# Three more chunks of an input projection as seven block products, and one block's selection moved between attention steps

## The reference, cut to what matters

```python
h = rmsnorm(x, g_mix_pre[l])
z = h @ w_in[l]                     # 1024 -> 3,908 columns
qa, ka, va, qi, ki, wi, qb, kb, vb, gb = split(z)
qa, ka, qi, ki, qb, kb = (rope(a, pos) for a in ...)
# group A, prompt, in blocks of 128 queries
sc = sum_h wi[h] * relu(qi[h] @ ki.T)          # indexer, 4 heads
sc = where(key <= query, sc, -inf)
_, sel = top_k(sc, 128)             # 128 keys for each query
a = softmax(qa @ ka[sel].T / 8) @ va[sel]      # 8 heads of 64
# group A, sample rows: the same over 256 cached keys and the new one, top 64
# group B: retention over qb, kb, vb in chunks of 128 tokens, gated by gb
x = x + rmsnorm(concat(a, b) @ w_out[l])
x = x + rmsnorm(relu(rmsnorm(x) @ w_up[l])**2 @ w_down[l])
```

## Time and profile before

| | us |
|---|---|
| median of three runs | 1571.54 |
| the profiled execution, its own time | 1573.14 |
| its span in the profile | 1571.4 |
| layer 0, start of chunk 1, and end of P7 of chunk 4 (attention begins) | 27.70, 163.06 |
| layer 0, chunk 5 ends, chunk 6 begins | 216.50 |
| layer 0, chunk 6's sample rows begin | 266.18 |
| layer 1, the same first two marks | 805.08, 942.78 |

### The profile page before, as it was taken

How to read it: one execution, slowest core, us unless ns; L and a number is a source line. 1 busy time by engine, 2 the same in 40 slices (tenths; PEclk the granted TensorE clock), 3 DMA queues, 4 the chain that set the end, 5 groups by cost and what they waited for, 6 DMA issues and landing times.

```text
span 1571.4 us, 21618 instructions
## 1 busy us (share of the span) xinstructions
PE 1547.7 (98%) x7966; PEld 1154.9 (73%) x7966; DVE 845.1 (54%) x1708; ACT 450.0 (29%) x1045; POOL 476.1 (30%) x354
## 2 busy tenths in 40 slices
PE   8999999999999999999999999999999999999998
PEld 5445755688888888888844466556888888888887
DVE  4599679846652013333467977788366610132334
ACT  5222355225421003310242224551253200123101
POOL 0005201023653424345310051010146524234461
PEclk9999999999999999999999999999999999999999
DMA  6326311024332122222223272110243421322211
GB/s 211 131 72 215 135 55 54 3 86 133 131 112 88 74 108 81 86 73 84 94 72 108 81 235 89 54 55 14 74 147 122 135 80 54 112 103 81 80 55 55
DMA packets 52811, 150.40 MB, mean 96 GB/s; under 512 B 8250, under 2 KB 29506, under 8 KB 39394
## 3 DMA queue, kind: packets, MB, share of 16 engines
q1 hardware_dynamic: 45218, 140.65, 26.1%
q10 hardware_dynamic: 7488, 8.36, 1.5%
HBM read 139.79 MB, written 9.02 MB: 95 GB/s over the span
## 4 chain that ended last, share of the span: by engine, by line
PE 77%; DVE 18%; issue 2%; ACT 2%; POOL 0%; DMA 0%; ACTq 0%; DVEq 0%; POOLq 0%
PE ps L1186 46%; PE ps L806 9%; PE ps L1124 7%; PE ps L843 4%; DVE arena L1870 3%; DVE top L1868 3%; PE ps L771 1%; DVE x_feat L2024 1%; PE ps L784 1%; DVE arena L1814 1%; DVE arena L1816 1%; PE ps L971 1%; DVE rstd_ffn L1812 1%; PE ps L1082 1%; PE ps L994 1%
## 5 line engine op out<-in xcount | busy, mean ns | idle before, releaser
L806 PE MATMUL ps<-wring,h_feat 128*128 128x512 f32 (+1 forms) x704 | 316.3, 586 | 2.8 <-ACT h_feat L1309 2.5
L1186 PE MATMUL ps<-arena,wring 128*128 128x256 f32 (+1 forms) x1280 | 285.8, 382 | 0.3 <-DVE arena L2108 0.3
L1186 PEld LDWEIGHTS ps<-arena,wring 128*128 128x128 f32 x1280 | 243.0, 190 | 37.7 <-DVE arena L2108 1.1
L806 PEld LDWEIGHTS ps<-wring,h_feat 128*128 128x128 f32 x704 | 124.7, 190 | 125.7 <-issue 112.5
L2405 POOL TENSOR_TENSOR wring<-wring,arena 128x512 f32<-128x512 f32 (+1 forms) x48 | 78.8, 1641 | 345.3 <-PE ps L1186 321.9
L1186 PE MATMUL ps<-h_feat,wring 128*128 128x256 f32 (+1 forms) x768 | 176.6, 381 | 0.0
L1186 PEld LDWEIGHTS ps<-h_feat,wring 128*128 128x128 f32 x768 | 145.9, 190 | 21.6
L1186 PE MATMUL ps<-mix,wring 128*128 128x256 f32 (+1 forms) x512 | 120.2, 383 | 0.8 <-DVE p_sb L2082 0.8
L1186 PE MATMUL ps<-arena 128*128 128x264 f32 x512 | 119.1, 386 | 0.0
L1124 PE MATMUL ps<-mix,wring 128*128 128x256 f32 (+1 forms) x512 | 115.1, 384 | 0.8 <-ACT mix L1473 0.8
L2388 POOL TENSOR_TENSOR pt_sb<-pt_sb 128x256 f32<-128x256 f32 (+1 forms) x94 | 72.8, 774 | 126.4 <-ACT pt_sb L1283 123.1
(11 more groups left out here) (251 smaller groups left out, 2041.8 us busy)
## 6 DMA issues: line engine op xcount, KB each, us to landing
wring<-in_w_all SPq DMA_DIRECT2D x108, 1024.0 KB, 5.1
arena<-in_cache_k SPq DMA_DIRECT2D x32, 256.0 KB, 5.2
arena<-in_cache_v SPq DMA_DIRECT2D x32, 256.0 KB, 4.4
o_k_out<-arena ACTq DMA_DIRECT2D x2, 1024.0 KB
o_v_out<-arena ACTq DMA_DIRECT2D x2, 1024.0 KB
arena<-in_state SPq DMA_DIRECT2D x2, 1024.0 KB, 4.8
o_rets_out<-arena ACTq DMA_DIRECT2D x2, 1024.0 KB, 9.8
wring<-in_w_idx SPq DMA_DIRECT2D x3, 648.0 KB, 4.9
```

Of the source, the lines that this page charges most:

```text
L806: last = mm(ps[:, bank_of(c, i), 0:width], h_feat[:, k, token_cols(t)], wt, start=(k == 0), stop=(k == KD - 1))
L1186: last = mm(out, a[:, j, :], b, start=(opens(n) and j == 0), stop=(j == nk - 1), skip_group_check=True)
```

## The change

`BLOCKED` becomes (1, 2, 3, 4, 5): chunks 1, 2 and 3 go by seven products as well. With that come their output sums on ACT and DVE, twelve more chunk sums and one more input sum on POOL in each layer (`in1` is formed twice, since its place is needed in between), and other buffers. The rotation of the sample rows goes ahead of those of the tokens, since their transposes are wanted earlier. Index transposes, dots and the other pieces beside PE get new places. POOL starts with the input sums instead of the keys. The 16 rounds on `sc[3]` and its mask leave the part ahead of attention; four rounds go to places 6 and 7 of chunk 4, twelve to the steps in chunk 5 (`LATE_ROUNDS`).

```diff
-BLOCKED = (4, 5)
+BLOCKED = (1, 2, 3, 4, 5)
+LATE_ROUNDS = [(1, 1), (1,), (1, 0), (1, 0), (1, 1), (1, 1), (1, 1), (1, 0)]
+DOTS = [(3, 2), (4, 0), (4, 6), (5, 4), (6, 2), (7, 0)]
...
-                project(1, beside_q)
-                project(2, beside_k)
-                project(3, beside_v)
+                project_blocks(1, beside_q)
+                project_blocks(2, beside_k)
+                project_blocks(3, beside_v)
...
             def beside_q(i, k):
-                if (i, k) == (0, KD - 1):
+                if (i, k) == (2, 3):
...
                     for c0, c1 in [(0, P), (P, 2 * P), (2 * P, 2 * P + HD)]:
                         transpose_group(zr[0], c0, c1)
...
-                if 1 <= i <= 3 and k % 4 == 1:
-                    j = 4 * (i - 1) + k // 2
+                if (i, k) in DOTS:
+                    j = 2 * DOTS.index((i, k))
...
             def beside_qb(i, k):
...
-                if (i, k) in ((3, KD - 1), (6, 5)):
+                if (i, k) in ((2, 3), (5, 3)):
...
             def beside(c, i, s):
 
+                if (c, i) in ((4, 6), (4, 7)) or c == 5 and s < len(LATE_ROUNDS[i]):
+                    n = {(4, 6): 1, (4, 7): 1}.get((c, i), LATE_ROUNDS[i][s])
+                    select_top(sc[3], top8[:], n)
+                if (c, i, s) == (5, 7, 1):
+                    block_mask(3)
...
-                rope(1, 0)
-                for j in range(3 * NI):
-                    combine(j)
-                    if j % 4 == 3:
-                        rope(1, 1 + j // 4)
-                rope(1, 4)
-                select_top(sc[1], top8[:], 6)
+                rope(1, NT)
+                for j in range(4):
+                    combine(j)
+                chunk_u2(1)
...
+                combine(10)
+                combine(11)
+                chunk_c12(1)
+                rope(1, 2)
+                rope(1, 3)
+                chunk_c21(1)
+                select_top(sc[1], top8[:], 1)
                 rope(1, 0)
+                rope(1, 1)
                 dve.wait_ge(ts_mm, past(ts_mm) + 1)
-                rope(2, 0)
+                rope(2, NT)
...
-                select_top(sc[3], top8[:], 9)
...
-                select_top(sc[3], top8[:], 2)
...
-                select_top(sc[3], top8[:], 4)
                 chunk_u2(4)
-                select_top(sc[3], top8[:], TOPK_P // 8 - 15)
-                block_mask(3)
+                select_top(sc[2], top8[:], TOPK_P // 8 - 13)
+                block_mask(2)
...
                 input_sum(1)
                 input_sum(2)
                 input_sum(3)
-                chunk_sum(4, 1)
-                chunk_sum(4, 2)
+                chunk_sum(1, 1)
+                chunk_sum(1, 2)
                 input_sum(4)
-                chunk_sum(4, 3)
-                chunk_sum(4, 4)
+                chunk_sum(1, 3)
+                chunk_sum(1, 4)
                 for n in range(1, 5):
-                    chunk_sum(5, n)
+                    chunk_sum(2, n)
+                chunk_sum(3, 1)
+                chunk_sum(3, 2)
```

More of the change, by code:

```diff
@@ L825, in project_blocks @@
                         pe.wait_ge(in_sums, past(in_sums) + 2)
+                    if n == 5 and c == BLOCKED[-1]:
+                        pe.wait_ge(in_sums, past(in_sums) + 5)
                     if n == 7:
@@ L964, in attend @@
                     pe.wait_ge(pt_ready, past(pt_ready) + j + 2)
+                    if j == 0:
+                        pe.wait_ge(proj_scaled, past(proj_scaled) + 3 * (BLOCKED.index(3) + 1))
                     if h == 0 and b >= 2:
@@ L1567, in _ @@
                 act.wait_ge(ts_read, up(ts_read))
-                for i in range(2, TILES):
-                    evacuate(2, i)
-                evacuate(3, 0)
-                evacuate(3, 1)
-                take_groups([kT[:, h, :] for h in range(4)])
+                act.wait_ge(sdot_mm, past(sdot_mm) + 1)
+                nc.scalar.activation(rs[:], ps[:, 2:4, 0:L], ACT.Relu).then_inc(srelu_done, 1)
+                act.wait_ge(srelu_done, up(srelu_done))
+                scale_quad(1, "21", proj_c21)
+                take_p1(2)
+                act.wait_ge(wm_mm, past(wm_mm) + 1)
+                nc.scalar.activation(wm[:], ps[:, 6, 64:64 + 2 * NB].rearrange("p (g b) -> p g b", g=2), ACT.Copy).then_inc(wm_ready, 1)
+                act.wait_ge(wm_ready, up(wm_ready))
+                evacuate(2, 1)
+                take_first(2)
+                take_groups([qT[:, h, :] for h in range(2)])
+                take_p5(2)
+                take_groups([qT[:, 2, :]])
                 act.wait_ge(ts_mm, past(ts_mm) + 3)
@@ L1575, in _ @@
                 act.wait_ge(ts_read, up(ts_read))
+                take_groups([qT[:, 3, :]])
+                scale_quad(2, "22", proj_c22)
+                scale_quad(2, "12", proj_c12)
+                take_p1(3)
+                scale_quad(2, "21", proj_c21)
+                evacuate(3, 1)
+                take_first(3)
+                take_groups([kT[:, h, :] for h in range(2)])
+                take_p5(3)
+                take_groups([kT[:, h, :] for h in range(2, 4)])
                 act.dma_start(k_out[bass.ds(l, 1)].rearrange("a (t p) n -> p (a t) n", p=P), zr[0][:, 0:NT, :]).then_inc(out_k, 16)
                 act.dma_start(ks_out[bass.ds(l, 1)].rearrange("a p n -> (a p) n"), zr[0][0:NB, NT, :]).then_inc(out_k, 16)
-                evacuate(3, 2)
-                evacuate(3, 3)
-                evacuate(3, 4)
                 for g in range(2):
@@ L2463, in _ @@
                 input_sum(3)
[L2464 to L2465 removed]
+                chunk_sum(1, 1)
+                chunk_sum(1, 2)
                 input_sum(4)
[L2467 to L2468 removed]
+                chunk_sum(1, 3)
+                chunk_sum(1, 4)
                 for n in range(1, 5):
[L2470 removed]
+                    chunk_sum(2, n)
+                chunk_sum(3, 1)
+                chunk_sum(3, 2)
+                for b in range(CSLOTS):
+                    new_key(b)
+                chunk_sum(3, 3)
+                for b in range(CSLOTS, NB):
+                    new_key(b)
+                chunk_sum(3, 4)
+                input_sum(5)
+                for c in (4, 5):
+                    for n in range(1, 5):
+                        chunk_sum(c, n)
                 pool.wait_ge(gains_in, past(gains_in) + 32)
```

180 lines of the change are left out of this document (109 added, 71 removed).

## The result

The changed kernel takes 1612.02 us (median of four runs, 1611.34 to 1613.12) against 1571.95 of the kernel before: a ratio of 1.0253, 95% interval 1.0235 to 1.0271. It is slower by 40 us, where +24.7 and a range up to 1607 were forecast. The sign was right, and PE does wait at the three places that the prediction names; the size was not right, and the time lies above the range.

A forecast was written before the change was run, and what follows sets the result against it. PE was taken to bound the kernel ahead of attention, DVE the attention stretch once rounds moved there. Layer terms of +11.9 and +12.8 gave +24.7 on 1573.14, so 1597.8, or 1596.2 on the median; range 1573 to 1607.

The forecast's parts named there:

- the three places that the prediction names: PE waits for rotations at the index transposes, at the start of chunk 2 and at its P7.
- Products: Chunks 1 to 3: seven products in place of direct matmuls save 3.4 us a chunk, -10.3 us in each layer.
- waits that go: Ahead of attention: small PE waits in layer 0, -1.0 us; in layer 1 a wait with slow clock, -3.4.
- the values moved ahead: The second group of cached values goes from inside the attention stretch to ahead of it, +1.9 us a layer.
- chunk 2 without holds: Start of chunk 2: DVE's two rotations and c21 take 5.4 us against 3.5, 1.5 late with no hold.
- Holds by POOL's sums: POOL sums delay DVE operations: index transposes +4.0 / +5.7 us, start of chunk 2 3.5, P7 of chunk 2 +2.0.
- The rounds between the steps: Attention stretch: 24.3 us of rounds, 14.5 hidden in DVE's waits for PE; +10.3 us a layer, bounds 0 and 24.8.
- Clock: One fall to half clock behind PE's new waits, in layer 1, +1.6 us; bounds 0 and 12.8.
- rival 4: PE's new waits of 2 to 6 us each bring a clock fall, eight instead of one: 1607 us; chance 0.07.
- Rival 1: POOL's sums hold DVE little at the three places: 1573 to 1583 us, put at 1580; chance 0.18.
- rival 2: No holds and no lateness at chunk 2's start; only products against selection count: 1571 us, no change; chance 0.08.
- rival 3: The moved rounds hide in DVE's waits during attention: 1554 us without holds, 1577 with them; chance 0.09.

The follow-up runs named there:

- run 2: Changed kernel with POOL writing short constants in place of the input sums and the chunk sums of chunks 1 to 3; 1582.4 us, ratio 1.0069.
- run 1: Kernel before with only the sixteen selection rounds on sc[3] and the mask moved between attention steps; 1599.1 us, ratio 1.0178.
- run 8: Changed kernel with POOL writing constants in place of the first four input sums and the sums of chunk 1 only; 1598.2 us, ratio 1.0169.
- run 4: Changed kernel with eight of the sixteen rounds ahead of attention again, eight still between the steps; 1604.8 us, ratio 1.0222.
- run 5: Changed kernel with eight rounds ahead of attention, the other eight where DVE of the kernel before had its waits; 1594.8 us, ratio 1.0143.
- run 11: Kernel before with seven rounds on sc[3] moved into DVE's gaps between attention steps, and the mask behind step 19; 1570.5 us, ratio 0.9991.
- run 3: Changed kernel with matmuls of no use ahead of four of PE's waits, into a free PSUM bank; 1609.2 us, ratio 1.0237.
- run 16: Changed kernel with constants in place of the same sums, written two and a half times to keep POOL busy about as long; 1583.4 us, ratio 1.0070.

## Why the prediction was wrong

Point by point, by the terms of its sum, layer 0 / layer 1:

- *Products, waits that go, the values moved ahead, chunk 2 without holds*: with no holds the terms give 135.4 - 10.3 - 1.0 + 1.9 + 1.5 = 127.5, and 137.7 - 10.3 - 3.4 + 1.9 + 1.5 = 127.4. Run 2 has 127.7 / 127.7. These terms were right in sum. The wait that run 2 keeps at the sample rows of chunk 2 is 1.9 us, which is 5.4 less 3.5; the prediction had rounded that to 1.5. The 3.4 in layer 1 were right for another reason than the one given: run 1 has 3.0 of them with ACT's list as it was.
- *Holds by POOL's sums, with the clock behind the waits*, the step that failed in size. Priced: 4.0 + 3.5 + 2.0 = 9.5, and 5.7 + 3.5 + 2.0 + 1.6 of clock = 12.8. (The 5.7 is 7.0 less 1.1, so 5.9; that changes nothing.) Measured (changed kernel minus run 2): 15.6 / 16.0. By PE's rows these are 10.1 / 12.7 us of waits and 5.4 / 3.3 us of the same matmuls at a lower clock. The waits came out 0.6 and 1.5 us above their price of 9.5 and 11.2; the larger miss is the slow clock, which had 0 / 1.6. By place: the input sums and those of chunk 1 cost 6.0 / 6.8 (run 8) for 4.0 / 5.7; all later ones 9.6 / 9.3 for 5.5. A hold was 2.05 and 2.03 us ahead of the transposes, where I had taken 1.76; two held rotations stand ahead of u2 of chunk 2, where I had counted one; and u2 of chunk 3 brought a wait of 1.0 where I had none. DVE was busy 117.5 us there in layer 0, against 95.6 in run 2: 22 us of holds (21 in layer 1), of which PE felt 16. The rotation of the sample rows, held three times ahead of the first combine, cost PE nothing that shows: DVE waits for ACT behind it.
- *The rounds between the steps*: +10.3 forecast, 12.9 / 12.8 measured, and 13.0 / 14.7 alone in run 1. The queue was the cause, as forecast. The 14.5 us of room were taken as one pool that fills to the end, and 2.6 us of them stayed empty. What lay among the rotations had no cover (runs 4, 5, 11); and in the stretch PE now waited up to 3.3 us at a time, with the slow clock behind.
- *Clock*: +1.6 in all. Cut into windows of 0.5 us, the changed kernel falls to 0.50 five times in layer 0 and three times in layer 1, eight falls for the one that I took. That is rival 4's count, and its 1607 us is the number nearest to the 1612. By itself the clock was a small part of the loss: run 3 filled four of the waits and took 2.8 us off, since DVE was late next anyway. The holds make PE late, and part of that lateness shows as waits and part as slow matmuls.

Sum of the misses: holds with their clock 6.1 + 3.2, rounds 2.6 + 2.5, products' side +0.5, the rest of the span -0.8: 14.1 of the 14.2 between 38.9 and 24.7. The first three are differences of the same stretches, so that they add up is no proof of the causes; those rest on runs 1, 2, 8 and 16.

Rival 1 (cheap holds) and rival 2 (nothing waits) are refuted by PE's waits and by run 2; rival 3 (the rounds hide) by run 1. The upper end of the range had room for eight falls of the clock or for longer holds, but not for both with the rounds 2.6 and 2.5 us above their price. The sentence of the Trainium skill on whole lengths ("SBUF — State Buffer", Who interferes with whom), cited in the prediction, gave 1604 us there in place of 1596.

What stays open: how the 9.6 / 9.3 divide among the later places. No run takes one of them alone. In layer 0 the waits there are 2.65 and 0.95 us at the start of chunk 2, 2.73 at its P7 and 0.98 at P7 of chunk 3, and two of the falls lie behind them. Why the same waits of 2.65 and 2.73 us have a fall behind them in layer 0 and none in layer 1 is open too.

## What to carry to other kernels

An engine's idle time is room only where it stands: cut the waits one by one, put moved work into them, and give nothing to the stretches between. When work is moved to GpSimd, list the VectorE operations that will run beside it, those with two SBUF inputs above all, take each as held until the GpSimd sum ends, and look for the ones that somebody waits for. A faster matmul scheme can be taken one chunk at a time; it pays while every maximum, rotation and partial sum that TensorE waits for stays ahead of selection work in VectorE's list.
